# Attention beside the value tiles, head norms and the branches' operands beside the last gate tiles

## The reference, cut to what matters

```python
h = rms_norm_2(x, mix_norm)
dq, dk, dv, fq, fk, fv, g_dil, g_diff = jnp.split(h @ w_in, idx, axis=-1)
# dq, dk: norm and rotation; three groups (window, dilation) of 4 heads each -> o_dil, 512 wide
# fq, fk: norm and rotation; 4 heads with two score matrices each:
a = p[:, :, 0] - lam * p[:, :, 1]
o_diff = a @ fv                                   # 4 heads x 256
o_diff = rms_norm_2(o_diff, diff_subln) * (1.0 - lam_init)
y = sigmoid(g_dil) * (o_dil @ w_dil_branch) + sigmoid(g_diff) * (o_diff @ w_diff_branch)
x = x + y @ w_out
```

## Time and profile before

| | us |
|---|---|
| median of 3 runs | 3477.34 (3475.15 to 3477.53) |
| the profiled execution, its own time | 3478.72 |
| span of its trace | 3476.9 |
| PE busy | 3408.7 |
| DVE busy | 2245.7 |
| ACT busy | 1725.6 |
| POOL busy | 589.7 |

### The profile page before, as it was taken

The page is one execution under the profiler, slowest core; times in us unless marked ns, Lnnn a source line. Parts: engine busy times, 40 slices in busy tenths (PEclk is TensorE's granted clock), DMA queues, the critical chain, the costliest instruction groups (busy, mean ns, idle before and its releaser), DMA issues.

```text
span 3476.9 us, 59047 instructions
## 1 busy us (share of the span) xinstructions
PE 3408.7 (98%) x19486; PEld 2958.2 (85%) x19486; DVE 2245.7 (65%) x2907; ACT 1725.6 (50%) x2541; POOL 589.7 (17%) x543
## 2 busy tenths in 40 slices
PE   8999989999999989999999999999989999999999
PEld 7888878888888878888888888888878888888888
DVE  7757677777754465655555588856668656555544
ACT  5444555555544454454444444444456544544443
POOL 1203121111100021111100057711100111111000
PEclk9999999999999999999999999999999999999999
DMA  5423545555566645555566654554446555555665
GB/s 195 151 97 116 177 137 187 187 191 185 191 185 190 189 138 193 187 187 187 187 191 184 216 171 169 190 185 159 163 134 195 184 193 187 187 188 186 191 187 172
DMA packets 174873, 616.03 MB, mean 177 GB/s; under 512 B 20657, under 2 KB 20817, under 8 KB 174417
## 3 DMA queue, kind: packets, MB, share of 16 engines
q1 hardware_dynamic: 174368, 609.84, 53.7%
q10 hardware_dynamic: 432, 5.24, 0.4%
HBM read 610.81 MB, written 4.19 MB: 177 GB/s over the span
## 4 chain that ended last, share of the span: by engine, by line
PE 87%; DVE 9%; issue 2%; ACT 1%; DMA 0%; POOL 0%; DVEq 0%; ACTq 0%; SPq 0%; POOLq 0%
PE acc L314 55%; PE acc L317 27%; DVE weights_low L264 3%; DVE x_T L2321 1%; DVE x_T L2319 0%; DMA weights_raw<-in_w_in 0%; DVE arena L2325 0%; PE ps_narrow L2111 0%; PE ps_wide L2087 0%; DVE arena L609 0%; DVE x_T L2323 0%; DVE halves_memory L609 0%; DVE x_T L2329 0%; ACT weights_high L257 0%; DVE arena L390 0%
## 5 line engine op out<-in xcount | busy, mean ns | idle before, releaser
L314 PE MATMUL acc<-moving_halves,weights_high 128*128 128x512 f32 x6592 | 2108.9, 401 | 14.9 <-DVE moving_halves L525 9.7
L264 DVE TENSOR_TENSOR weights_low<-weights_raw,weights_high 128x1024 fp32r<-128x1024 f32 (+1 forms) x1184 | 1442.6, 1231 | 758.5 <-ACT weights_high L257 756.8
L257 ACT ACTIVATE weights_high<-weights_raw 128x1024 fp32r<-128x1024 f32 (+1 forms) x1184 | 1221.7, 1033 | 816.1 <-PE acc L317 799.6
L317 PEld LDWEIGHTS acc<-moving_halves,weights_low 128*128 128x128 f32 x6592 | 1241.4, 188 | 292.8
L317 PE MATMUL acc<-moving_halves,weights_low 128*128 128x256 f32 x6592 | 1298.0, 278 | 0.0
L314 PEld LDWEIGHTS acc<-moving_halves,weights_high 128*128 128x128 f32 x6592 | 1012.2, 189 | 42.9 <-issue 26.4
L314 PE MATMUL acc<-gated_halves,weights_high 128*128 128x512 f32 x2112 | 663.3, 395 | 0.0
L384 ACT ACTIVATE cross_products<-acc 128x256 f32<-128x256 f32 x512 | 195.9, 383 | 715.9 <-PE acc L317 715.9
L317 PEld LDWEIGHTS acc<-gated_halves,weights_low 128*128 128x128 f32 x2112 | 396.8, 188 | 93.8
L407 POOL TENSOR_TENSOR stage_scratch<-unscaled,token_scale 128x256 f32<-128x256 f32 x264 | 216.9, 822 | 1251.3 <-DVE unscaled L390 792.9
L317 PE MATMUL acc<-gated_halves,weights_low 128*128 128x256 f32 x2112 | 414.9, 278 | 0.0
(11 more groups left out here) (327 smaller groups left out, 1737.5 us busy)
## 6 DMA issues: line engine op xcount, KB each, us to landing
weights_raw<-in_w_in SPq DMA_DIRECT2D x272, 512.0 KB, 3.8
weights_raw<-in_ffn_up SPq DMA_DIRECT2D x176, 512.0 KB, 4.0
weights_raw<-in_ffn_w_gate SPq DMA_DIRECT2D x176, 512.0 KB, 3.7
weights_raw<-in_ffn_w_up SPq DMA_DIRECT2D x176, 512.0 KB, 4.3
weights_raw<-in_ffn_w_down SPq DMA_DIRECT2D x160, 512.0 KB, 4.0
weights_raw<-in_ffn_down SPq DMA_DIRECT2D x80, 512.0 KB, 4.0
weights_raw<-in_w_out SPq DMA_DIRECT2D x64, 512.0 KB, 3.7
weights_raw<-in_ffn_w_down SPq DMA_DIRECT2D x32, 256.0 KB, 2.7
```

The source lines that it names most:

```text
L257: core.nc.scalar.activation(core.high[:, slot, 0:nk, :].rearrange("p a b -> p (a b)"), core.raw[:, slot, 0:nk * P], ACT.Copy).then_inc(cor ...
L264: core.nc.vector.tensor_tensor(core.low[:, slot, 0:nk, :].rearrange("p a b -> p (a b)"), core.raw[:, slot, 0:nk * P], core.high[:, slot, 0 ...
L314: core.nc.tensor.matmul(acc[:, bank, :, :], core.high[:, u % SLOTS, k, :], parts[:, prod.first[t] + k0 + k, :, :], start=(k0 + k == 0), st ...
L317: last = core.nc.tensor.matmul(acc[:, bank, 0, :], core.low[:, u % SLOTS, k, :], parts[:, prod.first[t] + k0 + k, 0, :], start=False, stop ...
```

## The change

Units start at body 24 instead of 30 (`FIRST = QK_BODIES + 4`), so six of them run beside value pairs; unit 15 runs beside body 39, its last two PE steps stand in body 40, and bodies 40 to 45 have 12 tiles, `turn` 0 to 11. Over these the head norms are spread: squares at turn 1 (ACT, two instructions, by halves of the heads), their sum at turn 2 (new, DVE), the sum over partitions at turn 3 (PE, four matmuls instead of eight), variance at turn 4, the root at turn 5, the Newton step at turn 6, the two multiplications at turn 8 (now from FQ to FK). The operand parts of the branches are made at turns 2 to 5 (one tile each) and 9 to 11 (three, three, two), and go to a place of their own in the arena. `y`, `z` and `gate` go to `halves_memory`.

```diff
-        self.y_parts = self.over(self.arena_at + KT * S * 4, "branch_halves", KT)
+        self.y_parts = self.over(self.arena_at + 28 * S * 4, "gated_branch_halves", KT)
...
     def sum_squares(self, pe):
-        pe.wait_ge(self.sq_ready, 1)
+        pe.wait_ge(self.sq_ready, 3)
         for h in range(HEADS):
-            for e in range(2):
-                last = self.nc.tensor.matmul(self.p_s[:, h, :], self.core.c("ones"), self.proj[:, FK + 2 * h + e, :],
-                                             start=(e == 0), stop=(e == 1))
+            last = self.nc.tensor.matmul(self.p_s[:, h, :], self.core.c("ones"), self.proj[:, DV + h, :],
+                                         start=True, stop=True)
...
+    def square_heads(self, act):
         act.wait_ge(self.out_done, len(self.UNITS))
-        self.nc.scalar.activation(proj[:, FK:FK + 8, :], proj[:, FQ:FQ + 8, :], ACT.Square).then_inc(self.sq_ready, 1)
+        for e in range(2):
+            heads = self.proj[:, FQ:FQ + 8, :].rearrange("p (h e) s -> p h e s", e=2)[:, :, e, :]
+            self.nc.scalar.activation(self.proj[:, DV + 4 * e:DV + 4 * e + 4, :], heads, ACT.Square).then_inc(self.sq_ready, 1)
+
+    def root_heads(self, act):
         act.wait_ge(self.var_ready, 1)
...
+    def add_halves(self, dve):
+        dve.wait_ge(self.sq_ready, 2)
+        self.nc.vector.tensor_tensor(self.proj[:, DV:DV + 4, :], self.proj[:, DV:DV + 4, :], self.proj[:, DV + 4:DV + 8, :],
+                                     ALU.add).then_inc(self.sq_ready, 1)
...
+class Branches:
...
+    def high(self, act, ks):
+        for k in ks:
+            if k == 4:
+                act.wait_ge(self.attention.normed, 2)
+            if k == 10:
+                act.wait_ge(self.core.part_low, self.base + 4)
+            self.core.nc.scalar.activation(self.parts[:, k, 0, :], self.sources[k], ACT.Copy).then_inc(self.core.part_high, 1)
+
+    def low(self, dve, ks):
+        for k in ks:
+            dve.wait_ge(self.core.part_high, self.base + k + 1)
+            if k == 4:
+                dve.wait_ge(self.attention.normed, 2)
+            self.core.nc.vector.tensor_tensor(self.parts[:, k, 1, :], self.sources[k],
+                                              self.parts[:, k, 0, :].bitcast(F32),
+                                              ALU.subtract).then_inc(self.core.part_low, 1)
...
-    FIRST = QK_BODIES + V_BODIES
-    assert prod.bodies - FIRST == len(attention.UNITS)
+    FIRST = QK_BODIES + 4
+    UNITS, LAST_V, DIL_UNITS = len(attention.UNITS), QK_BODIES + V_BODIES, HEADS * HALVES
+    branches = Branches(core, proj, attention, branch_parts)
+    SPLIT_AT = {2: (0,), 3: (1,), 4: (2,), 5: (3,), 9: (4, 5, 6), 10: (7, 8, 9), 11: (10, 11)}
+    assert prod.bodies - FIRST - UNITS == 6
...
-        attention.take_probs(act, n)
-        attention.take_out(act, n)
-        attention.finish_act(act)
+                if turn == 1:
+                    attention.square_heads(act)
+                if turn == 5:
+                    attention.root_heads(act)
+                branches.high(act, SPLIT_AT.get(turn, ()))
...
-        attention.finish_dve(dve, chain)
+                if turn == 2:
+                    attention.add_halves(dve)
+                if turn == 4:
+                    attention.variance(dve)
+                if turn == 6:
+                    attention.refine_root(dve, chain)
+                if turn == 8:
+                    attention.normed_heads(dve)
+                branches.low(dve, SPLIT_AT.get(turn, ()))
...
                 if t == 0:
-                    if n:
+                    if 0 < n <= UNITS:
                         attention.transpose_probs(pe, n - 1)
-                    attention.scores(pe, n)
-                elif n:
+                    if n < UNITS:
+                        attention.scores(pe, n)
+                elif 0 < n <= UNITS:
                     if n == 1:
+                        pe.wait_ge(vt_out, 6)
+                    if n == DIL_UNITS + 1:
                         pe.wait_ge(vt_out, V_BODIES + 1)
                     attention.weigh_values(pe, n - 1)
-        attention.transpose_probs(pe, n)
-        attention.weigh_values(pe, n)
-        attention.sum_squares(pe)
+                if turn == 3:
+                    attention.sum_squares(pe)
...
-    operand = Given(core, [proj[:, t, :] for t in (*range(DQ, DQ + 4), *range(FQ, FQ + 8))])
-    free = core.h_mem[:, 12:16, :, :].rearrange("p k c s -> p (k c) s")
-    z, gate = free[:, 0:4, :], free[:, 4:8, :]
+    free = core.h_mem[:, :, :, :].rearrange("p k c s -> p (k c) s")
+    y, z, gate = free[:, 0:16, :], free[:, 24:28, :], free[:, 28:32, :]
...
         act.dma_start(core.x[:, :, :], core.d["x_kept"]).then_inc(x_back, 16)
-        act.wait_ge(attention.normed, 2)
-        operand.act(act)
         nc.scalar.preload_act_table(ACT.Sigmoid)
         act.wait_ge(core.z_free, gates_scaled + 2)
...
-        operand.dve(dve)
```

More of the change, by code:

```diff
@@ L2057, in __init__ @@
         self.p_t, self.p_o = core.wide[1], core.narrow
+        self.roots, self.variances, self.spare = (proj[:, DV + j:DV + j + 4, :] for j in (8, 12, 16))
     @staticmethod
@@ L2200, in finish_dve, with refine_root @@
         dve.wait_ge(self.sum_done, 1)
-        var, y = proj[:, FK + 4:FK + 8, :], proj[:, FK:FK + 4, :]
-        nc.vector.tensor_scalar(var, self.p_s[:, :, :], 1.0 / (2 * HD), EPS, ALU.mult, ALU.add).then_inc(self.var_ready, 1)
+        self.nc.vector.tensor_scalar(self.variances, self.p_s[:, :, :], 1.0 / (2 * HD), EPS, ALU.mult,
+                                     ALU.add).then_inc(self.var_ready, 1)
+    def refine_root(self, dve, chain):
         dve.wait_ge(self.rooted, 1)
-        newton_rsqrt(nc, chain, y, var, proj[:, DK:DK + 4, :])
+        newton_rsqrt(self.nc, chain, self.roots, self.variances, self.spare)
@@ L2205, in finish_dve, with normed_heads @@
+    def normed_heads(self, dve):
         for e in range(2):
[L2206 to L2211 removed]
+            src, out = (self.proj[:, at:at + 8, :].rearrange("p (h e) s -> p h e s", e=2)[:, :, e, :] for at in (FQ, FK))
+            self.nc.vector.scalar_tensor_tensor(out, src, self.lam[:, 1 + e:2 + e], self.roots, ALU.mult,
+                                                ALU.mult).then_inc(self.normed, 1)
@@ new lines, with __init__, on @@
+class Branches:
+    N = 12
+    def __init__(self, core, proj, attention, parts):
+        self.core, self.attention, self.parts, self.base = core, attention, parts, core.parts
+        self.sources = [proj[:, t, :] for t in (*range(DQ, DQ + 4), *range(FK, FK + 8))]
+        core.parts += self.N
+    def high(self, act, ks):
[13 more added lines that the diff above has]
+                                              ALU.subtract).then_inc(self.core.part_low, 1)
+    def on(self, pe):
+        return lambda t, k: pe.wait_ge(self.core.part_low, self.base + k + 1)
@@ L2216, in mix_in_stage @@
+def mix_in_stage(core, prod, operand_of, proj, trig, lam, branch_parts, following):
     nc = core.nc
@@ L2358, in vector @@
             for i, t in walk(FIRST + n, FIRST + n + 1):
+                turn = 2 * (n - UNITS) + t
                 take_for_scaling(core, dve, prod, acc, i, t)
-                if t == 0:
+                if n < UNITS and t == 0:
                     attention.take_scores(dve, chain, n)
-                else:
+                elif n < UNITS:
                     attention.normalize(dve, chain, n)
-        attention.finish_dve(dve, chain)
+                if turn == 2:
[7 more added lines that the diff above has]
+                branches.low(dve, SPLIT_AT.get(turn, ()))
     def gpsimd(pool):
@@ L2573, in whole @@
         p_in2 = proj_product("w_in_2", MIX_TILES).place(core, scaled=True, unscaled=DV)
-        p_branch = Product(KT // 2, [4, 8, 4, 8], branch_source, first=[0, 4, 0, 4]).place(core)
+        branch_parts = core.over(core.arena_at + 4 * S * 4, "branch_halves", Branches.N)
+        p_branch = Product(KT // 2, [4, 8, 4, 8], branch_source, first=[0, 4, 0, 4], parts=branch_parts).place(core)
         p_out2 = proj_product("w_out_2", KT, parts=y_parts).place(core)
@@ L2594, in whole @@
         down1 = product_add_stage(core, p_down1, 0.5, p_in2, "mix_norm", after_gated())
-        mix_in, attention = mix_in_stage(core, p_in2, lambda: Normed(core, "mix_norm", "prepared"), core.arena, core.trig,
-                                         core.lam, p_branch)
-        branch = branch_stage(core, p_branch, core.arena, y_parts, p_out2, attention, x_back, y_low)
+        mix_in, branches = mix_in_stage(core, p_in2, lambda: Normed(core, "mix_norm", "prepared"), core.arena, core.trig,
+                                        core.lam, branch_parts, p_branch)
+        branch = branch_stage(core, p_branch, core.arena, y_parts, p_out2, branches, x_back, y_low)
         w_out2 = product_add_stage(core, p_out2, 1.0, p_up2, "ffn2_norm",
```

35 lines of the change are left out of this document (15 added, 20 removed).

## The result

| | before | after |
|---|---|---|
| median, us | 3477.44 of 4 (3475.15 to 3482.32) | 3455.9 of 4 (3451.86 to 3458.24) |
| ratio after/before, 95% interval | | 0.9934, 0.9922 to 0.9945 |
| profiled execution, its own time | 3478.72 | 3455.51 |
| its span | 3476.9 | 3453.7 |

A forecast was written before the change was run, and what follows sets the result against it. PE, busy 98% of the span, was taken as the bound, with DVE bounding the branch stage. The take moves from 2581.10 to 2559.9, other terms zero, so the median 3477.3 - 21.2 = 3456.1 us; range 3454 to 3462.

The forecast's parts named there:

- The hole: Gap on PE between the last gate matmul and the first branch matmul, 23.08 us, expected to go.
- The ruler: DVE's take of tile 1, branch body 0, start of its unbroken run: 2581.10 before, forecast 2559.9, 21.2 us gained.
- E: End of PE's last `mix_in` (gate) matmul: 2551.8 before, forecast 2554.6.
- PE's moved work: PE's remaining work moves into the gate bodies and lengthens them: 1.11 for unit 15, 1.72 for sums; E moves 2.8 us.
- Unit 15: ... together 1.11: Unit 15's PE work moved into gate bodies: two transposes at 0.11 and 8 value matmuls at 0.89.
- Six value pairs share bodies with units ... only reordered: zero: In the six shared bodies, 0.44 us of transposes and unit steps are only reordered; 4.4 us spare at the probabilities; zero cost.
- Everything beside the 12 last tiles costs nothing: DVE and ACT work beside the last 12 gate tiles: zero, hidden by weight slots, 8.3 us against 5.9 at worst.
- DVE bounds the branch stage: In the branch stage DVE's chain sets the body, 9.03 us, against 8.34 that PE needs for 24 blocks.
- Moved buffers of `y`, `z` and `gate`: same shapes, same engines, zero: Moving these three buffers was claimed to change no time: zero.
- Rival 1: Part comes back at branch start, POOL held or chunk late behind the residual: 5.6 us, gain 15.6, 3461.7; chance 0.12.
- Rivals 2 and 3: Bodies 40 to 45: DVE bursts reach PE, 3468.9, chance 0.05; six shared bodies: PE waits at probability transposes, slower, 0.02.
- Rival 4: The end doesn't move: DVE bounds the branch stage and absorbs PE's earlier start; 3477, chance 0.03.

## Why the prediction was right

The mechanism was right and so was the number, with terms that were off by up to 1 us and in part cancelled. That the median came within 0.2 us of the forecast is luck: four runs of the changed kernel went from 3451.86 to 3458.24.

- **The hole goes, and little is late behind it**: PE's first branch matmul follows within 0.1 us, at full clock, as said. The ruler was put at E + 5.3 and came at E + 5.12. ACT's queue, not PE, is late there, as said: with the table load gone the take came 0.5 earlier.
- **PE's moved work**: 2.83 us was worked out, E moved by 3.33 (it ends at 2553.7 and not past 2554.6 because this execution reached the last rotation 1.4 us earlier). Of the two terms the sums measured 1.73, for 1.72:

```profile
2507.36 1.73 PE ps_wide L2119 x8
```

So the other term, "Unit 15: ... together 1.11", carries the half microsecond; the run with the units alone had 1.58 for it. The term forgot a piece of work. Unit n's value product stands beside body n + 1, so in the kernel before unit 14's stood behind the last gate tile, past E = 2551.8, and moved ahead of it too:

```profile
2551.59 0.60 PE L2111 MATMUL ps_narrow<-stage_scratch,arena 128*128 128x128 f32 x4
```

Four matmuls at 0.11 are 0.44, and 1.11 + 0.44 is 1.55. It lengthens the gate bodies by as much as it shortens what lies behind E, so it changes the two stretches and not their sum. "Six value pairs share bodies with units ... only reordered: zero" held to the hundredth: from one cross part on ACT to the same one a body later, the bodies with a whole dilated unit took 13.15 and 14.12 us beside gate tiles before, and 13.59 and 14.56 beside value pairs, the 0.44 of the transposes more.
- **Everything beside the 12 last tiles costs nothing**: right. Turn 6, called the worst, in DVE's timeline:

```profile
2526.61 0.42 DVE L390 TENSOR_TENSOR unscaled<-acc,cross_products 128x256 f32<-128x256 f32 x1
2526.94 1.21 DVE L1050 TENSOR_TENSOR arena<-arena 128x1024 f32<-128x1024 f32 x1
2528.19 1.64 DVE L1051 SCALAR_TENSOR_TENSOR arena<-arena 128x1024 f32<-128x1024 f32 x1
2529.86 1.23 DVE L1052 SCALAR_TENSOR_TENSOR arena<-arena 128x1024 f32<-128x1024 f32 x1
2531.12 2.36 DVE L264 TENSOR_TENSOR weights_low<-weights_raw,weights_high 128x1024 fp32r<-128x1024 f32 x2
```

From the take's start to the first subtraction's end it is 5.7 us, from the take's end 5.3; the Newton step takes 4.2 of them, for 3 x 1.24 = 3.7. Its second instruction is the long one, 1.64, beside a scaling on POOL that started at 2527.20 and took 1.54 where most take 0.75. The prediction had POOL late at moved steps; that DVE's own step grows too it had not. The two longer bursts, with waits of 0.6 and 8.2, show that the slack is real and ends near where it was put.
- **DVE bounds the branch stage**, so the ruler is its take: right, shown from both sides by the sums left out and doubled. The body's length was wrong, though: 9.03 was carried over from the earlier trace rows, and the changed kernel's chain has

```profile
2586.52 1.22 DVE weights_low L264
2595.42 1.22 DVE weights_low L264
2604.33 1.22 DVE weights_low L264
```

That is 8.9, a tenth less a body, near 0.9 us in all. "Moved buffers of `y`, `z` and `gate`: same shapes, same engines, zero" is the step that missed it. The variants that keep this stage's code, with the units alone among them, have 8.91 too, so it came with the new places or code of the stage and not with the moved work. By the views of waits the kernel before has six waits of DVE's products behind its takes there (1.6 us in all, 2585 to 2645) that the changed kernel hasn't; why they are gone stays open.
- **The sum**: 1.4 of the 23.2 us of span lie ahead of the change. Behind E the take gained 24.21 where 24.03 was expected (21.2 and the 2.83 of E), and E took 0.5 more, so at the ruler it is 20.9 against 21.2. The shorter bodies, 0.97, which the prediction didn't have, bring it to 21.9.
- **Rival 1, part comes back at the branch start**: its first half didn't happen. POOL's last scaling took 0.75 and ended at 2555.57, before ACT asked for it. Its second half is real and was nearly met: "slack of 2.5 us on the chunk" was a slack of about zero, because the term used the median landing of 3.5 us. In windows with a DMA share of 1.05 and 0.93 the landing was 5.9. It cost nothing only since ACT's table load delayed the need for it.
- **Rivals 2 and 3** did not occur: no PE wait at a weight beside the turns, none at L2098. Rival 2's mechanism exists and needs 2 us more in a turn. **Rival 4** is refuted by the stage's 25.18 us.
- **The lower clock.** The loss of half clock in the hole was costed at nothing on top, since it was inside the measured 23.08; with the units alone it reappeared as 3.78 us of sums in place of 1.73.

## What to carry to other kernels

A hole that the bound engine has between two stages is worth what fills it, less what the filled work adds to that engine, and the measure is the first unbroken run of whichever engine bounds the next stage. Work may be hidden beside tiles up to the depth of the buffers (here three chunks, 8.0 us as measured); past that it comes back one to one, and a little more through the clock. A small leftover at the new seam (here 0.5 us of a table load) may be covering something else, so look for what is just in time before removing it, and let a big transfer start away from where small ones are urgent. Work handed from the engine that bounds a stage to an idle neighbour gains only what the neighbour doesn't give back by lengthening the bound engine's other instructions (here 1.1 of 1.14 us).

## What the runs showed of the hardware that was not expected

- A 2 MB load on ACT's queue stretched a 512 KB weight chunk from 3.4 us to 5.9 and 6.1, at a DMA share of 0.93 to 1.05 and 380 to 393 GB/s.
- A 128x256 sum on POOL took 0.77 us (0.75 to 0.85 over the stage) when it started first and 1.55 when DVE's 128x1024 subtraction had; the subtraction took 1.22 when first and 1.77 when second.
- PE's granted clock stayed 1.00 over a wait of 3.4 us, read 0.74 over the window around one of 8.2, and fell to 0.50 in the hole of 18.8.
